# Rotary partners of the second projection: four DMAs per tile on SyncE's queue instead of a swap matmul

## The reference

```python
def apply_rope(x, cos, sin):
    x1, x2 = jnp.split(x, 2, axis=-1)
    return jnp.concatenate([x1 * c - x2 * s, x2 * c + x1 * s], axis=-1)

def second_block(...):
    cos, sin = rope_tables(positions, HEAD_DIM)
    h = rms_norm_2(x, g_mix[l])
    proj = h @ w_in[l]
    qa, ka, va, qd, kd, vd = jnp.split(proj, splits, axis=-1)
    qa = apply_rope(qa.reshape(...), cos, sin)
    out_a = sliding_window_sink_attention(qa, ka, va, sinks[l])
    od = differential_attention(qd, kd, vd, lam)
    x = x + jnp.concatenate([out_a, out_b], axis=-1) @ w_out[l]
    ...
```

## Time and profile before

| | us |
|---|---|
| median of 3 runs | 1080.33 |
| lowest and highest | 1079.66, 1080.83 |
| span of the profiled execution | 1072.5 |
| TensorE matmuls busy | 1008.9 (94%) |
| VectorE busy | 691.5 (64%) |
| ScalarE busy | 533.3 (50%) |
| second projection, TensorE's first unit to VectorE's last sum | 685.7 to 744.7 |

### The profile page before, as it was taken

One profiled execution on the slowest core, in us unless ns is written; L12 is line 12 of the kernel. 1 busy time (PEld: TensorE's weight loads), 2 busy tenths in 40 slices (PEclk: granted clock), 3 DMA queues, 4 the chain that ended last, 5 costly groups with the idle time before them and its releaser, 6 DMA issues.

```text
span 1072.5 us, 16586 instructions
## 1 busy us (share of the span) xinstructions
PE 1008.9 (94%) x5680; PEld 859.9 (80%) x5680; DVE 691.5 (64%) x1087; ACT 533.3 (50%) x948; POOL 69.9 (7%) x78
## 2 busy tenths in 40 slices
PE   6999999998799899999999989998999999999997
PEld 5888888786698886788888877887877878888885
DVE  4766666669894763666666577487636537666664
ACT  6655555567221222655555474644745545445542
POOL 3002000002140420000000000000300000000000
PEclk9999999999899999999999999999899999999999
DMA  7777666454210100576656745455034236666661
GB/s 214 218 237 211 191 194 186 114 141 115 79 41 1 40 2 3 174 210 183 192 178 192 229 137 161 135 169 165 20 99 126 91 98 185 194 183 184 194 194 61
DMA packets 204892, 153.93 MB, mean 144 GB/s; under 512 B 5947, under 2 KB 190624, under 8 KB 204848
## 3 DMA queue, kind: packets, MB, share of 16 engines
q1 hardware_dynamic: 203760, 151.35, 47.2%
q0 software_dynamic: 1088, 2.00, 0.7%
HBM read 152.28 MB, written 1.05 MB: 143 GB/s over the span
## 4 chain that ended last, share of the span: by engine, by line
PE 81%; DVE 10%; ACT 5%; issue 2%; DMA 2%; DVEq 0%; SPq 0%; ACTq 0%
PE ps L453 80%; DVE wlo L1340 2%; DMA raw<-in_w_ckv 1%; ACT arena L986 1%; DVE XT L1369 1%; DVE X L1388 1%; ACT whi L965 1%; ACT XT L996 0%; DVE arena L1577 0%; DVE arena L1455 0%; DMA CON<-in_consts 0%; DMA raw<-in_ffn_w_gate 0%; ACT arena L1206 0%; DVE arena L1581 0%; DVE arena L1585 0%
## 5 line engine op out<-in xcount | busy, mean ns | idle before, releaser
L453 PE MATMUL ps<-XT,whi 128*128 128x512 f32 x1440 | 518.6, 402 | 5.3 <-DVE XT L1369 5.3
L1340 DVE TENSOR_TENSOR wlo<-raw,whi 128x1024 fp32r<-128x1024 f32 x280 | 338.8, 1230 | 117.2 <-ACT whi L965 97.0
L453 PE MATMUL ps<-XT,wlo 128*128 128x256 f32 x1440 | 404.5, 281 | 0.0
L453 PEld LDWEIGHTS ps<-XT,whi 128*128 128x128 f32 x1440 | 271.3, 188 | 72.7 <-issue 5.3
L965 ACT ACTIVATE whi<-raw 128x1024 fp32r<-128x1024 f32 x280 | 293.3, 1055 | 45.9 <-PE ps L453 18.3
L453 PEld LDWEIGHTS ps<-XT,wlo 128*128 128x128 f32 x1440 | 272.6, 189 | 3.6 <-issue 0.4
L453 PE MATMUL ps<-whi,H 128*128 128x512 f32 x608 | 176.8, 393 | 1.8 <-DVE H L1415 1.6
L453 PE MATMUL ps<-arena 128*128 128x128 f32 (+7 forms) x1192 | 147.2, 294 | 15.0 <-DVE arena L1581 5.4
L453 PEld LDWEIGHTS ps<-arena 128*128 128x128 f32 (+3 forms) x1192 | 134.5, 189 | 29.4 <-DVE arena L1581 5.8
L453 PEld LDWEIGHTS ps<-whi,H 128*128 128x128 f32 x608 | 108.8, 188 | 25.4 <-DVE H L1415 2.3
L453 PE MATMUL ps<-wlo,H 128*128 128x512 f32 x304 | 94.7, 393 | 0.0
(11 more groups left out here) (227 smaller groups left out, 749.2 us busy)
## 6 DMA issues: line engine op xcount, KB each, us to landing
raw<-in_ffn_w_gate SPq DMA_DIRECT2D x44, 512.0 KB, 4.5
raw<-in_ffn_w_up SPq DMA_DIRECT2D x44, 512.0 KB, 3.9
raw<-in_ffn_w_down SPq DMA_DIRECT2D x44, 512.0 KB, 4.6
raw<-in_w_in SPq DMA_DIRECT2D x36, 512.0 KB, 3.8
raw<-in_w_up SPq DMA_DIRECT2D x32, 512.0 KB, 4.6
raw<-in_w_down SPq DMA_DIRECT2D x32, 512.0 KB, 3.4
raw<-in_w_out SPq DMA_DIRECT2D x16, 512.0 KB, 3.4
raw<-in_w_ckv SPq DMA_DIRECT2D x16, 512.0 KB, 4.8
```

The lines of the kernel that those rows point to most:

```text
L453: return pe.matmul(o, st, mv, start=start, stop=stop, skip_group_check=True)
L1340: dve.tensor_tensor(wlo[:, n % RING, :], raw[:, n % RAW, :], whi[:, n % RING, :].bitcast(F32), sub).then_inc(lo_ready, 1)
```

## The change

The swap matmuls are taken out. A buffer RSW of two tiles takes the partners, in space that the preceding stage's value tiles leave. SyncE, on the queue of the weight loads, waits for the sum of tile k and for its buffer to be free (the rope two before), and issues four DMAs of 32 partitions x 256 values each, that exchange neighbouring groups of 32 partitions; these stand behind the load of weight unit k+7 in its program. VectorE waits for all four ahead of both products, and its second product reads the partner from RSW instead of PSUM. KSW is filled by two DMAs of 64 partitions that follow the partners of tile 11 and wait for the rope of tile 4. TensorE waits for a sum only where a value tile is transposed, and ahead of the scores for all ropes and for KSW. VectorE's copy to KSW goes too.

```diff
--- before.py
+++ after.py
@@ -242,6 +242,7 @@
         KSW = ar(4608, T)
         RC, RSN = ar(4864, T), ar(5120, T)
         RT = ar(5376, 2, T)
+        RSW = ar(24064, 2, T)
         VT2 = ar(5888, NT, 640)
         SC = ar(7168, 12, 512)
         POSI, POSF, ANG = (ar(9216 + 256 * k, T) for k in range(3))
@@ -310,8 +311,9 @@
         pooled, pool_mm, pool_hi, mid_upd = \
             sems("pooled pool_mm pool_hi mid_upd")
 
-        rope_arg, rope_tab, lam_arg, lam_exp, q_low, q_sum, rope_mm, rope_done = \
-            sems("rope_arg rope_tab lam_arg lam_exp q_low q_sum rope_mm rope_done")
+        rope_arg, rope_tab, lam_arg, lam_exp, q_low, q_sum, key_swap, rope_done = \
+            sems("rope_arg rope_tab lam_arg lam_exp q_low q_sum key_swap rope_done")
+        rope_swap = [ctx.enter_context(nc.semaphore(f"rope_swap{i}")) for i in range(2)]
         vt_mm, vt_ev, sc_mm, sc_sum, sc_max, sc_exp, p_ready, pt_mm = \
             sems("vt_mm vt_ev sc_mm sc_sum sc_max sc_exp p_ready pt_mm")
         pt_ev, pv_mm, o_hi, rec_ready, cp_ready, od_ss, od_std, od_norm, odt_mm = \
@@ -351,6 +353,7 @@
                  [[(j, m, 0) for m in range(4)] for j in (4, 5)] + \
                  [[(j, m, kb) for m in range(2) for kb in range(2)] for j in (6, 8)] + \
                  [[(10, m, 0) for m in range(4)]]
+        ROPED = [k for k in range(14) if k != 5]
         W_BANKS, Q_BANKS, C_BANKS = (4, 5, 2, 3), (4, 5, 0, 1), (4, 5, 6, 7)
 
         ORDER = list(range(6, 12)) + list(range(6))
@@ -419,10 +422,30 @@
             sp.dma_start(SNK, t["sinks_2"].broadcast_to([P, 8])).then_inc(pos_in, 16)
             for i in range(N_CKV):
                 load(B_CKV + i, 0, cols("w_ckv_2", i * P))
+            def partners(k):
+
+                n = ROPED.index(k)
+                sp.wait_ge(q_sum, k + 1)
+                if n >= 2:
+                    sp.wait_ge(rope_done, n - 1)
+                else:
+                    sp.wait_ge(ct_mm, KC)
+                for a in range(0, P, 32):
+                    sp.dma_start(RSW[a:a + 32, n % 2, :], QKV[a ^ 32:(a ^ 32) + 32, k, :]).then_inc(rope_swap[n % 2], 16)
+
             for i in range(N_WIN2):
                 load(B_WIN2 + i, 0, cols("w_in_2", i * P))
+                if i >= 7 and i - 7 in ROPED:
+                    partners(i - 7)
             for c in range(KC):
                 load(B_WOUT2 + c, 0, rows("w_out_2")[:, c:c + 1, :])
+                k = c + N_WIN2 - 7
+                if k in ROPED:
+                    partners(k)
+                if c == 0:
+                    sp.wait_ge(rope_done, ROPED.index(4) + 1)
+                    for b in range(2):
+                        sp.dma_start(KSW[64 * b:64 * b + 64, :], QKV[64 - 64 * b:128 - 64 * b, 4, :]).then_inc(key_swap, 16)
             for i in range(KC):
                 load(B_CQ + i, 0, cols("w_cq_2", i * P))
             for c in range(KC):
@@ -761,32 +784,23 @@
                 pe.wait_ge(ct_ev, KC)
                 norm_t("mix2")
 
-                n_rope = n_vt = 0
+                n_vt = 0
                 for i in range(N_WIN2 + 1):
                     if i < N_WIN2:
                         if i >= 4:
                             pe.wait_ge(q_sum, i - 3)
                         a_unit(B_WIN2 + i, 0, PS[Q_BANKS[i % 4]], None if i else "mix2")
                     k = i - 1
-                    if k < 0:
-                        continue
-                    pe.wait_ge(q_sum, k + 1)
-
                     if k == 5 or k >= 14:
+                        pe.wait_ge(q_sum, k + 1)
                         if n_vt >= 2:
                             pe.wait_ge(vt_ev, n_vt - 1)
                         for tt in range(NT):
                             last = pe.transpose(PS[7 - 4 * (n_vt % 2)][:, tt * P:(tt + 1) * P], QKV[:, k, tt * P:(tt + 1) * P], ident)
                         last.then_inc(vt_mm, 1)
                         n_vt += 1
-                    else:
-                        if n_rope >= 2:
-                            pe.wait_ge(rope_done, n_rope - 1)
-                        mm(PS[6 - 4 * (n_rope % 2)][:, 0:T], con("swap32"), QKV[:, k, :]).then_inc(rope_mm, 1)
-                        n_rope += 1
-                pe.wait_ge(rope_done, n_rope)
-                mm(PS[6][:, 0:T], con("swap64"), QKV[:, 4, :]).then_inc(rope_mm, 1)
-                pe.wait_ge(rope_done, n_rope + 1)
+                pe.wait_ge(rope_done, len(ROPED))
+                pe.wait_ge(key_swap, 16 * 2)
                 pe.wait_ge(vt_ev, 5)
 
                 def scores(k):
@@ -1726,17 +1740,15 @@
                                 own.next())
                             dve.wait_ge(own_dve, own.n)
                             dve.tensor_scalar(NLAM, NLAM, -LAM_INIT, None, add).then_inc(own_dve, own.next())
-                        dve.wait_ge(rope_mm, n_rope + 1)
+                        dve.wait_ge(rope_swap[n_rope % 2], 16 * 4 * (n_rope // 2 + 1))
                         dve.wait_ge(q_sum, k + 1)
                         if n_rope:
                             dve.wait_ge(rope_done, n_rope)
                         dve.tensor_tensor(RT[:, 0, :], QKV[:, k, :], RC, mul).then_inc(own_dve, own.next())
-                        dve.tensor_tensor(RT[:, 1, :], PS[6 - 4 * (n_rope % 2)][:, 0:T], RSN, mul).then_inc(own_dve, own.next())
+                        dve.tensor_tensor(RT[:, 1, :], RSW[:, n_rope % 2, :], RSN, mul).then_inc(own_dve, own.next())
                         dve.wait_ge(own_dve, own.n)
                         dve.tensor_tensor(QKV[:, k, :], RT[:, 0, :], RT[:, 1, :], add).then_inc(rope_done, 1)
                         n_rope += 1
-                dve.wait_ge(rope_mm, n_rope + 1)
-                dve.tensor_copy(KSW, PS[6][:, 0:T]).then_inc(rope_done, 1)
                 split_to(B_WOUT2 + RING)
 
                 dve.tensor_scalar(NSNK, SNK, -1.0, None, mul).then_inc(own_dve, own.next())
```

## The result

The changed kernel takes 1084.64 us, the median of 9 runs between 1078.63 and 1091.94; the kernel before took 1080.12 in 9 runs on the same chips. The ratio is 1.0052, with an interval from 1.0034 to 1.0070: slower by 5.6 us (3.7 to 7.6); the two medians lie 4.5 apart. The forecast was 1082.9, in a range of 1077.5 to 1087.5. From the end of sum 0 to the end of sum 17 the projection takes 62.97 us, where it took 54.94: 8.0 more.

A forecast was written before the change was run, and what follows sets the result against it. TensorE bounds the projection before, the loop through the partner fetch after. Six fetches (6L = 23.4) less 22.6 give +0.9 us, a half clock +1.7, together +2.6 on 1080.33: 1082.9, range 1077.5 to 1087.5.

The forecast's parts named there:

- The bound: Projection: passes from TensorE, 3.25 us a unit, to a loop through the partner fetch and VectorE, 3.35 each.
- The loop's own time: VectorE from the start of a rope to the end of the next sum but one: 2.73 us.
- The fetch, L: Time from the end of a tile's sum until its partner has landed: 3.97 us behind a w_in load, 3.57 behind w_out.
- the queue's limit: Fetch behind the load just ahead on the same queue: -0.33 + 3.8 + 0.5 = 3.97 us, taken as the larger limit.
- a sign of being wrong: Projection: the prediction called itself wrong if weight splits wait for raw weights.
- This step: SyncE's issues in the projection: occupied 2.4 us of 3.3, so weight loads add nothing.
- The end of the stage: From sum 14 to the last sum: 7.0 us, plus 1.7 for a half clock on units 16 and 17.
- The tail: After the last sum: moves unchanged as a block; swap64 and the copy to KSW cost nothing.
- the forecast's own case: Whole kernel: slower, 1081 to 1085 us; the forecast with its clock stretch had chance 0.45.
- the slow fetch of the rivals: Partner transfers cost more behind a load than their bytes: L = 4.65, +7.0 with the clock, 1087.3 us; chance 0.16.
- My own sign of being wrong: Projection: the prediction called itself wrong if sums are over 3.6 us apart.
- Hidden fetch: Partner transfers do not queue behind the load's packets: L = 3.1 to 3.3, -3.4 us, 1076.9; chance 0.17.

The follow-up runs named there:

- e1: The kernel before without its 14 swap matmuls and with nothing in their place, so the partner exchange is left out: 1071.95 us.
- e2: The changed kernel with each tile's four partner transfers issued ahead of the weight load instead of behind it: 1083.19 us.
- e4: The changed kernel itself, unedited, run and profiled a second time: 1087.66 us.
- e3: The changed kernel with only two of the four partner transfers per tile, so half the partners are stale: 1081.02 us.
- e9: The changed kernel with partner transfers ahead of the load and only two of four issued per tile: 1073.88 us.
- e5: The changed kernel with the rope one unit later and four partner buffers instead of two, transfers still on SyncE: 1077.83 us.
- e10: The changed kernel with dummy matmuls where TensorE waits for tiles 5 (8 of them) and 14 (16): 1085.55 us.
- e7: The changed kernel with the four partner transfers issued by GpSimd instead of SyncE, rope lag and buffers unchanged: 1087.87 us.
- e6: The changed kernel with the rope one unit later, four partner buffers, and GpSimd issuing the partner transfers: 1073.15 us.

## Why the prediction was right, and what was mis-sized

**The bound.** Right, as to what took it over. The swaps cost TensorE 0.43 us each (5.35 us of stage in e1, 5.6 forecast), and the bound passed to the loop of sum, fetch, rope, split and second sum. The loop's own time of 2.73 us holds: in the changed kernel the rope of tile 6 starts at 724.95 and sum 8 ends at 727.65, 2.70 later. That the loop closes over every second sum is only half of it. Up to tile 6 the chain runs over the even tiles, then it passes through SyncE to tile 7, whose issues stood behind tile 6's, and goes on over tiles 9 and 11 to 12. At tiles 8 and 10 VectorE came late by itself and waited little for the partner:

```profile
732.22 0.42 DVE L1747 TENSOR_TENSOR arena<-arena 128x256 f32<-128x256 f32 x1 [0.25 <-DMA arena<-arena]
739.43 0.42 DVE L1747 TENSOR_TENSOR arena<-arena 128x256 f32<-128x256 f32 x1 [0.20 <-DMA arena<-arena]
```

The count over even tiles below still gives the right total, since every even sum still ends 2.7 us after the rope two units before it starts.

**The fetch, L.** This is the term that was mis-sized. The forecast had 3.97 us (six of them 23.4); the profile has 4.44, 4.34, 4.59, 4.58, 4.52 and 5.39 for tiles 2, 4, 6, 8, 10 and 12, together 27.9, which is 4.4 us more of stage. Each input was low by a little. A row for the four transfers of tile 6 (us from issue to landing), and one for all loads in the stage:

```profile
DMA to landing us min/median/max: 2.6/3.1/3.6
```

```profile
DMA to landing us min/median/max: 3.3/4.0/4.5
```

The loads land after 4.0 us instead of 3.8; the load ahead of tile 6's partners was issued at 720.05. The issues take 0.59 and stand 0.58 to 0.64 apart, not 0.5 (chain above), so the fourth was issued at 722.37, 2.0 us after the sum and not 1.6, and landed 2.6 us later, which is the upper end that I had from the 512 KB store. By measured inputs the queue's limit is -0.3 + 4.0 + 0.5 = 4.2 us and the issues' 2.0 + 2.6 = 4.6: they end close together, and the larger is not the one that I took (the 2.6 itself holds some of the load ahead: without it the last landed in 1.9, e2). That fits the stages, 3.3 us shorter than e4's in e2 (the load no longer ahead), 6.1 in e3 (two issues fewer), and 11.9 in e9 (both), more than the two together.

**SyncE.** I wrote that it is occupied 2.4 us of 3.3 and that the loads add nothing. The loads indeed do not stand in the chain for their weights, though ScalarE's splits waited for raw weights, 12.8 us in seven waits where the kernel before has none in this stage; I had named such waits as a sign of being wrong. But SyncE is occupied 3.1 us per rotated tile, and where a sum follows the last in 2.6 to 3.0 us its fetch queues there: 5.12 us for tile 3, 5.98 for tile 7. The two issues for KSW (L448), which I had cost at nothing, push tile 12's to 5.39, 0.9 more than tile 10's; they stand in the chain between the partners of tile 11 and the load ahead of tile 12's:

```profile
741.19 0.59 SPq L434
741.83 0.59 SPq L448
742.47 0.60 SPq L448
743.11 0.58 SPq L372
```

This step failed: it took SyncE to have room. e5, where the loop over three units is short enough, shows the price: 2.9 us of stage above e1.

**The end of the stage.** From sum 14 on I had 7.0 us and 1.7 for the clock; it took 10.0. I had left out that sum 15 stands behind rope 13 and its fetch. With the clock kept up (e10) it takes 8.1, so the fetch of tile 13 is worth about 1.1 and the half clock about 1.9. That it would fall on units 16 and 17 after an idle time of 5 us was right: idle 5.6 us, half clock from 749.5 to 756.4. The idle time ahead of tile 5 was 3.4 us, not 2.5, and brought the other stretch at half clock, which I had not foreseen; e4 has none there and the same stage, so no price of it is seen.

**The tail** (swap64, KSW's copy) was right: from sum 17 to the end of the last split it is 4.3 us before and after (760.19 to 764.45).

**The numbers.** In the stage the forecast's +2.6 became +8.0: 4.4 by the fetch, 1.3 by the end, 0.3 the other way because the loop's own time was 2.69 us and not 2.73. The runs' median moved by 4.5 us in one set, where 1084.64 fell into the forecast's own case of 1081 to 1085, and by 8.6 in another: e4's 1087.66 lies just above the whole range. So that the time met the forecast's case is in part luck. By the fetch (L of 4.3 and more) and the stage, the slow fetch of the rivals (+7.0) is the case that came. My own sign of being wrong, sums over 3.6 us apart, came too: the pairs from sum 2 to sum 12 stand 7.0 to 7.3 us apart, the last 8.1, which makes 3.67 a unit. I also read the 7.8 us between the profile's span and the runs' median as start and end; each run's time lies only 1.7 to 2.1 above its own span, and the rest is that this profile's execution reached the stage early (last section). The sum starts from the median, so it is not moved. Hidden fetch is refuted (it needed L under 3.4), and so is the estimate from the Trainium skill's DMA: Bandwidth & Descriptors (Anatomy of one DMA): its 2.0 us fixed is near the 1.8 us of the quickest partner transfer in the profile, but the L of 3.7 that I worked out from it is 0.6 to 0.9 too short, as it had no load ahead and too quick an issue.

## What to carry to other kernels

A small transfer that is fetched inside a loop of dependent work costs its whole path: the issues ahead of it on its sequencer, the large transfers ahead of it on its queue, its landing. Count them against the number of periods that the consumer leaves, not against the bandwidth. Against e1's stage the same 52 transfers cost 13.4 us with one unit of lead on SyncE, 2.9 with two, and next to nothing with two and an issuing engine of their own. The second unit alone does not do it where the issuer itself is full, and another issuer alone (e7) does nothing. An engine that is off the path only by a few tens of per cent (VectorE at 2.6 us of 3.25) leaves no room for such a wait in its program order.

## What the runs showed of the hardware

**Instruction packets beside the fetches.** In e4 the rope of tile 6 waited 4.9 us. Its four transfers and the DMA queues from 720.2 to 721.1 us:

```profile
DMA to landing us min/median/max: 2.6/3.3/4.3
```

```profile
q1 hardware_dynamic: 146, 0.08, 34.2%
q8 instruction: 1, 0.02, 6.1%
```

The packet list of the trace has one instruction packet of 16 KB in that time, on one DMA engine, from 720.21 for 0.88 us. Of the 64 increments that the four transfers owe, 61 had arrived by 720.81, the last three came at 722.33, 722.59 and 722.85. In the changed kernel such a packet (726.41, for 1.24 us) falls on the fetch of tile 7, whose last transfer takes 3.72 us to land, where those of tiles 2, 4 and 8 take 2.3 to 2.6. The kernel before has one in the stage as well (714.83) and its sums stay 3.25 us apart there. The Trainium skill's DMA: Bandwidth & Descriptors (Why a DMA increments its semaphore by 16) has each engine of a transfer count for itself, so that only the full count means landed; the late last increments agree with that. That the packet causes the late landing is not shown. Loads filled the engines just then too (DMA share 0.92 and 1.09 from 721.1 to 722.9 in e4), and in e7 the partners of tile 6 landed 4.35 us after their last issue, before the next such packet began.

What the packets go with in every profile is a long issue. In the 13 profiles SyncE's issues between 685 and 765 us take at most 0.70 us, but for 15 that take 0.75 to 1.49; each of the 15 begins during a 16 KB instruction packet, right behind another issue. A load's issue that begins during one after a pause takes its usual 0.33 to 0.37, and GpSimd's issues (e6, e7) are no longer there than elsewhere. The partner issues of e2, min/median/max in ns, with the long one of 1.47 us at 721.99 inside a packet that lasts from 721.60 to 723.00:

```profile
L434 SPq DMA_DIRECT2D arena<-arena x52: 507/590/1472, 692.9 to 743.0; - x52
```

**The same code takes different times ahead of the stage.** Over the 13 profiles the end of sum 0 lies between 689.3 and 697.2 us, and by and large later with more time at half clock ahead of it: 24 us in the two earliest, 44 in the latest. The kernel before spreads by itself (689.8 and 693.5 in its two profiles), and e4 is the changed kernel at 692.9, so it is not the change that brings it. Most of the half clock lies between 200 and 415 us, in the first block, whose code is the same in all (0.96 against 0.91 granted from 235 to 440 us in the two first profiles). It is why a single profile's span says little here: the changed kernel's 17.7 us more of span are 7.5 from there, 8.0 from the stage and 2.2 behind it.
